# Spreading a norm's inverse root over the partitions: a transpose of the repeated column in place of a product with the identity

## The chip, the core and the metric

The kernel runs on one core of a Trainium2 chip. The metric is device time in microseconds (us) of one execution, the median over several runs. Lower is better.

## The reference, cut to what matters

Three residual blocks of a language model run one after the other on 256 tokens of width 1024: a state-space mixer, a latent-attention mixer, and a block with sparse attention, a gated convolution, a feed-forward part and a per-layer gate. Every block begins with a root-mean-square norm, and there are more norms inside:

```python
def rms_norm(x, w):
    xf = x.astype(jnp.float32)
    return (xf * lax.rsqrt(jnp.mean(xf * xf, axis=-1, keepdims=True) + RMS_EPS)).astype(x.dtype) * w

def reference(x, ...):
    h = x
    h = h + ssd_mixer(rms_norm(h, norm_w[0]), ...)   # 8 grouped norms of its own inside
    h = h + mla_mixer(rms_norm(h, norm_w[1]), ...)   # one norm of the queries, one of the keys
    x = rms_norm(h, final_norm_w)
    ...                                              # sparse attention, conv with layer norm, ffn, gate
    return rmsnorm(h, g_final)
```

The change touches only how the inverse root of a norm gets to where it is multiplied in. No weight, no activation and no other product is touched.

## The kernel before, in words

Activations lie feature-major: a tile is 128 features (partitions) by 256 tokens (columns), and 1024 features are eight such tiles. The weights stream through the core once, in slabs of eight 128x128 blocks (512 KB). SyncE loads a slab into `raw` (six buffers), ScalarE rounds it to `wh` (line 1122), GpSimd takes the rest, `wl = raw - wh` (line 571, six buffers each), and TensorE multiplies. A `project` on TensorE is, for each block of 128 input features, three products of a 128x128 block with 128x256 activations: lines 628, 629 and 630 (high by high, high by low, low by high). Eight such blocks make one output tile of the usual kind. Lines 635 to 637 do the same with the activations as the stationary side. Vector and scalar engines take each output out of PSUM, where three banks rotate, and prepare the next inputs.

Each engine's program is written out by hand, in one fixed order, with semaphores between the engines. TensorE's waits are on `wl_ready` (the slab is there), `proj_done` and the evacuation counts (the bank is free), and on the results of the small steps between the projections.

A norm needs one number for each token, while tokens lie along the columns of every partition. It goes like this:

- `norm_sum` on TensorE (line 655; `group_sum`, line 665, for the grouped norms): the squares are summed over the partitions, with the squares as the stationary side, which leaves one column of 128 sums for each half of the tokens, with the token on the partition.
- `inverse_root` on VectorE (lines 1589 to 1592, then 1567 to 1572): a Newton iteration for the inverse root of that column, in `root` (128 partitions, one column for each half of the tokens; `root1` and `late_tok` for two of the norms).
- `norm_spread` on TensorE (line 673): the column is repeated 128 times as the stationary side, the identity `ident` (in the tile `cst`) is the moving side, and the result holds the root of token j in column j of every partition. This is done for each half of the tokens, into PSUM.
- VectorE either copies it to `late` (line 1604), which later multiplies projection outputs, or multiplies it in at once (line 1557).

`norm_spread` is called 17 times, once with four columns (the last of the grouped norms, which holds two groups) and otherwise with two, so for 36 columns. Sixteen of the calls stand between products of a projection or of an attention stage: for six grouped norms it comes right after `head_out` (lines 756 and 757), in nine other places between ordinary work, and once with four columns within the first state-space output projections. The seventeenth comes at the end of the program (`n_fin2`), where nothing is left to project. There the same column is spread a second time, into another bank (line 1094), for ScalarE: it copies that to `late` (line 1533), GpSimd multiplies the last two of eight output tiles with it (line 589), and VectorE multiplies the first six with the first copy (line 1557). SyncE then stores the eight tiles in four transfers (line 560), the pair of GpSimd third and VectorE's last pair fourth.

Several other places of this kernel turn a 128x128 f32 tile with `nc.tensor.transpose`, which has the tile as the stationary side and the same identity as the moving side: lines 724 (`x_transpose`), 863 (`prob_transpose`), 931 (the gates), 997 (`unit_transpose`) and 1017 (`cmp_transpose`).

Of the kernel before, what the change touches and what calls it, by code (L numbers as in the profile page):

```python
# [18 lines left out]
P = 128  # L19
# [247 lines left out]
def build(nc, slabs_dram, vec_dram, const_dram, x_dram, p_dram, out_dram):  # L267
# [6 lines left out]
    with ctx:  # L274
        def sb(name, shape, dt=f32):
            return ctx.enter_context(nc.sbuf_tensor(name, shape, dt))
# [15 lines left out]
        msq, root, step = sb("msq", [P, 2 * TB]), sb("root", [P, 2 * TB]), sb("step", [P, 2 * TB])  # L292
# [4 lines left out]
        ident = cst[:, 0:128]  # L297
# [103 lines left out]
        PS_TR, PS_S, PS_Y, PS_M = psum[3], [psum[4], psum[5]], psum[6], psum[7]  # L401
# [47 lines left out]
        def sem(name):  # L449
            if name not in sems:  # L450
                sems[name] = ctx.enter_context(nc.semaphore(name))
            return sems[name]
# [140 lines left out]
        def _(pe):  # L593
# [75 lines left out]
            def norm_spread(n):  # L669

                pe.wait_ge(sem("norm_root"), n.i + 1)
                for b in range(n.groups * TB):
                    ins = nc.tensor.matmul(n.rstd[:, b * P:(b + 1) * P], n.root[:, b:b + 1].broadcast_to([P, P]), ident,  # L673
                                           start=True, stop=True)
                ins.then_inc(sem("norm_spread"), 1)

            def norm(n):
                norm_sum(n)
                norm_spread(n)
# [21 lines left out]
            for c in range(SSM_CT):  # L701
                project(f"xbc{c}", u, u_lo)
                if c == 0:
                    norm_sum(n_ssm)
                elif c == 1:
                    pe.wait_ge(sem("const_in"), 16)
                    norm_spread(n_ssm)
                if c == 19:

                    pe.wait_ge(sem("dt_scan"), 8)  # L710
                    pe.wait_ge(sem("masks"), 1)
                    for i, src in enumerate((dtT, acr)):
                        for b in range(TB):
                            o = PS_TR[:, (2 * i + b) * SSM_H:(2 * i + b + 1) * SSM_H]
                            ins = nc.tensor.transpose(o, src[0:SSM_H, b * P:(b + 1) * P], ident[0:SSM_H, 0:SSM_H])
                    ins.then_inc(sem("dt_tr"), 1)
# [48 lines left out]
            for j in range(SSM_PAIRS - 1):  # L765
                project(f"sz{j + 1}", u, u_lo)
                if j % 2:
                    cb_scores((j + 1) // 2)
                x_transpose(j + 1)
                decay_pair(2 * j + 2)  # L770
                head_out(2 * j)
                head_out(2 * j + 1)
                if j % 2 and j >= 3:

                    wait(pe, "cb_evac", (j + 3) // 2)
                    group_sum((j - 3) // 2)
                if j % 2 == 0 and j >= 4:
                    norm_spread(n_grp[(j - 4) // 2])
# [151 lines left out]
            for b in range(TB):  # L930
                ins = nc.tensor.transpose(PS_TR[:, b * P:(b + 1) * P], gT[:, b * P:(b + 1) * P], ident)
# [9 lines left out]
            for n in range(2):  # L941
                ins = nc.tensor.transpose(PS_TR[:, n * P:(n + 1) * P], hg[:, n * P:(n + 1) * P], ident)
# [144 lines left out]
            for b in range(TB):  # L1087
                c = slice(b * P, (b + 1) * P)
                nc.tensor.matmul(PS_M[:, b:b + 1], n_fin2.sum[:, c], ones[:, 0:1], start=True, stop=False)
                ins = nc.tensor.matmul(PS_M[:, b:b + 1], n_fin2.sqb(KD - 1)[:, c], ones[:, 0:1], start=False, stop=True)  # L1090
            ins.then_inc(sem("norm_sum"), 1)
            norm_spread(n_fin2)
            for b in range(TB):
                ins = nc.tensor.matmul(PS_TR[:, b * P:(b + 1) * P], root[:, b:b + 1].broadcast_to([P, P]), ident,
                                       start=True, stop=True)
            ins.then_inc(sem("final_spread"), 1)


# [1244 lines left out]
```

## Time and profile before

| | |
|---|---|
| median of 3 runs | 867.47 us (866.96 to 868.33) |
| span of the profiled execution, first to last instruction | 865.4 us, so the median is 2.1 us above it |
| TensorE busy | 847.8 us, 98% of the span, 7055 products |
| VectorE, ScalarE, GpSimd busy | 526.8, 485.7, 624.1 us |
| mean granted TensorE clock | 0.994 of full speed |

The profiled execution has no device time of its own listed beside its span; what lies around the span is taken as those 2.1 us. A matmul's end in the profile is modelled and products overlap in the pipeline, so what a product costs in a stream is the distance between the starts of products and not the duration of one.

### The profile page before, as it was taken

Reading aid. Unit: us, or ns where it says so; the run is one execution under the profiler, and the core shown is the slowest. Engines: PE = TensorE matmul, PEld = TensorE weight load, DVE = VectorE, ACT = ScalarE, POOL = GpSimd, SP = SyncE. Lnnn points to the kernel's source line nnn. Section 1 sums busy time; section 2 is a strip of 40 time slices with the busy share of each in tenths; the row PEclk is TensorE's granted clock in tenths of the full one; section 3 lists DMA queues with packets and bytes.
Section 4 is the critical chain, followed back from the end, with each engine's and each line's share of the span. In section 5 each row is a group of like instructions: output and inputs, shape, how many; then the busy total and the mean of one; then the engine's idle time right before and its main releaser. Section 6 shows DMA issues by size and latency. Waiting matters only on the chain.

```text
span 865.4 us, 18278 instructions
## 1 busy us (share of the span) xinstructions
PE 847.8 (98%) x7055; PEld 816.2 (94%) x7055; DVE 526.8 (61%) x1543; ACT 485.7 (56%) x925; POOL 624.1 (72%) x282
## 2 busy tenths in 40 slices
PE   8999999999999999999999999999999999999995
PEld 8999988889998899999999999988999999999995
DVE  5997758883243535445458998875566676641164
ACT  6755476664446456563846457875644544554361
POOL 4899756655997455563979899455868888889680
PEclk9999999999999999999999999999999999999997
DMA  8666633332774343433566577433646666667511
GB/s 331 192 219 218 193 99 98 99 98 75 220 218 155 114 145 107 140 99 122 162 204 190 180 210 222 127 95 116 184 144 204 177 192 182 187 193 221 170 49 50
DMA packets 38678, 138.46 MB, mean 160 GB/s; under 512 B 4416, under 2 KB 4544, under 8 KB 38592
## 3 DMA queue, kind: packets, MB, share of 16 engines
q1 hardware_dynamic: 38592, 137.30, 51.9%
q8 instruction: 56, 0.92, 0.5%
q14 instruction: 30, 0.25, 0.1%
HBM read 136.23 MB, written 1.05 MB: 159 GB/s over the span
## 4 chain that ended last, share of the span: by engine, by line
PE 80%; DVE 4%; issue 2%; ACT 1%; POOLq 0%; POOL 0%; ACTq 0%; DVEq 0%
PE ps L628 22%; PE ps L629 22%; PE ps L630 21%; DVE ps L1720 1%; PE ps L850 1%; PE ps L756 1%; PE ps L673 1%; PE ps L655 1%; PE ps L637 1%; PE ps L635 1%; PE ps L636 1%; PE ps L874 1%; PE ps L983 1%; PE ps L846 1%; PE ps L821 1%
## 5 line engine op out<-in xcount | busy, mean ns | idle before, releaser
L571 POOL TENSOR_TENSOR wl<-raw,wh 128x1024 fp32r<-128x1024 f32 x254 | 606.9, 2413 | 199.1 <-ACT wh L1122 198.9
L628 PE MATMUL ps<-uh,wh 128*128 128x256 f32 (+1 forms) x1248 | 352.4, 282 | 1.9 <-POOL wl L571 0.8
L629 PE MATMUL ps<-ul,wh 128*128 128x256 f32 (+1 forms) x1248 | 348.7, 279 | 0.0
L630 PE MATMUL ps<-uh,wl 128*128 128x256 f32 (+1 forms) x1248 | 348.3, 279 | 0.0
L1122 ACT ACTIVATE wh<-raw 128x1024 fp32r<-128x1024 f32 (+1 forms) x255 | 262.9, 1052 | 85.8 <-PE ps L630 77.9
L628 PEld LDWEIGHTS ps<-uh,wh 128*128 128x128 f32 (+1 forms) x1248 | 233.8, 187 | 3.7 <-issue 1.6
L629 PEld LDWEIGHTS ps<-ul,wh 128*128 128x128 f32 (+1 forms) x1248 | 233.7, 187 | 0.0
L630 PEld LDWEIGHTS ps<-uh,wl 128*128 128x128 f32 (+1 forms) x1248 | 233.2, 187 | 0.1
L1813 DVE TENSOR_TENSOR h<-ps,h 128x256 f32<-128x256 f32 x32 | 13.6, 425 | 103.8 <-PE ps L630 103.7
L629 PE MATMUL ps<-ffl,wh 128*128 128x256 f32 x176 | 49.3, 280 | 0.0
L628 PE MATMUL ps<-ffh,wh 128*128 128x256 f32 x176 | 49.1, 279 | 0.0
L630 PE MATMUL ps<-ffh,wl 128*128 128x256 f32 x176 | 49.1, 279 | 0.0
L1720 DVE SCALAR_TENSOR_TENSOR ps<-cpad,vec,ps 128x256 f32<-128x256 f32 x120 | 48.6, 480 | 0.0
L1611 DVE TENSOR_TENSOR fraw<-ps,late 128x256 f32<-128x256 f32 x44 | 18.4, 421 | 38.7 <-PE ps L630 38.6
L1720 DVE SCALAR_TENSOR_TENSOR ps<-sraw,vec,ps 128x256 f32<-128x256 f32 x96 | 38.9, 478 | 0.0
L1720 DVE SCALAR_TENSOR_TENSOR ps<-fraw,vec,ps 128x256 f32<-128x256 f32 x88 | 38.1, 481 | 0.0
L628 PE MATMUL ps<-ynh,wh 128*128 128x256 f32 x128 | 36.1, 282 | 0.0
L628 PE MATMUL ps<-ogh,wh 128*128 128x256 f32 x128 | 36.1, 282 | 0.0
L630 PE MATMUL ps<-ynh,wl 128*128 128x256 f32 x128 | 35.8, 280 | 0.0
L629 PE MATMUL ps<-ynl,wh 128*128 128x256 f32 x128 | 35.7, 279 | 0.0
L630 PE MATMUL ps<-ogh,wl 128*128 128x256 f32 x128 | 35.7, 279 | 0.0
L629 PE MATMUL ps<-ogl,wh 128*128 128x256 f32 x128 | 35.6, 278 | 0.0
(363 smaller groups left out, 1690.8 us busy)
## 6 DMA issues: line engine op xcount, KB each, us to landing
raw<-slabs SPq DMA_DIRECT2D x255, 512.0 KB, 4.0
h<-x_fm SPq DMA_DIRECT2D x4, 256.0 KB, 4.1
out_fm<-outb SPq DMA_DIRECT2D x4, 256.0 KB, 2.2
cst<-shape_consts SPq DMA_DIRECT2D x1, 768.0 KB, 8.4
vec<-vectors SPq DMA_DIRECT2D x1, 299.5 KB, 8.6
pin<-p_fm SPq DMA_DIRECT2D x1, 256.0 KB, 3.8
raw<-slabs SPq DMA_DIRECT2D x1, 128.0 KB, 2.8
vec<-vectors SPq DMA_DIRECT2D x1, 4.0 KB, 2.4
```

The costliest lines, as they stand in the source:

```text
L571: nc.gpsimd.tensor_tensor(wl[:, s % PART_RING, :], raw[:, s % RAW_RING, :], wh[:, s % PART_RING, :].bitcast(f32), ALU.subtract).then_inc(s ...
L628: nc.tensor.matmul(res, w_h, a_h, start=first, stop=False)
L629: nc.tensor.matmul(res, w_h, a_l, start=False, stop=False)
L630: ins = nc.tensor.matmul(res, w_l, a_h, start=False, stop=last)
L635: nc.tensor.matmul(res, a_h, w_h, start=first, stop=False)
L636: nc.tensor.matmul(res, a_h, w_l, start=False, stop=False)
L637: ins = nc.tensor.matmul(res, a_l, w_h, start=False, stop=last)
L655: ins = nc.tensor.matmul(PS_M[:, n.col + c:n.col + c + 1], src[:, b * P:(b + 1) * P], ones[:, 0:1], start=n.summed or k == g * per, stop=n ...
L1122: nc.scalar.activation(wh[:, s % PART_RING, 0:n], raw[:, s % RAW_RING, 0:n], ACT.Copy)\
L1611: tt(dst, o[0:rows, 0:T], late[0:rows, :], ALU.mult).then_inc(sem("dve_evac"), 1)
L1720: return stt(dst, src, w, dst, ALU.mult, ALU.add)
L1813: tt(h[:, k, :], o[:, 0:T], h[:, k, :], ALU.add).then_inc(sem("dve_evac"), 1)
```

## The change

Both places that spread a root over the partitions call `nc.tensor.transpose` in place of `nc.tensor.matmul`. The operands are the same: the repeated column is the stationary side, the identity the moving side, the same slice of PSUM the result. No wait, no semaphore and no other instruction changes, and each engine's instructions keep their order.

```diff
@@ norm_spread
                 pe.wait_ge(sem("norm_root"), n.i + 1)
                 for b in range(n.groups * TB):
-                    ins = nc.tensor.matmul(n.rstd[:, b * P:(b + 1) * P], n.root[:, b:b + 1].broadcast_to([P, P]), ident,
-                                           start=True, stop=True)
+                    ins = nc.tensor.transpose(n.rstd[:, b * P:(b + 1) * P], n.root[:, b:b + 1].broadcast_to([P, P]), ident)
                 ins.then_inc(sem("norm_spread"), 1)
@@ the end of the program
             norm_spread(n_fin2)
             for b in range(TB):
-                ins = nc.tensor.matmul(PS_TR[:, b * P:(b + 1) * P], root[:, b:b + 1].broadcast_to([P, P]), ident,
-                                       start=True, stop=True)
+                ins = nc.tensor.transpose(PS_TR[:, b * P:(b + 1) * P], root[:, b:b + 1].broadcast_to([P, P]), ident)
             ins.then_inc(sem("final_spread"), 1)
```

## Rows read from the trace of the kernel before

**Rows 1.** The page: the span, and TensorE's busy time, share and products.

```profile
span 865.4 us, 18278 instructions
PE 847.8 (98%) x7055; PEld 816.2 (94%) x7055; DVE 526.8 (61%) x1543; ACT 485.7 (56%) x925; POOL 624.1 (72%) x282
```

**Rows 2.** Busy time by stage: stretch, length, busy us (xcount) by engine, clock, DMA.

```profile
530.00:852.00 322.00, 320.88 (x2741) 313.36 (x2740) 187.97 (x556) 176.54 (x330) 239.89 (x101) 1.00 0.53 158
852.00:865.40 13.40, 3.75 (x18) 3.27 (x16) 6.27 (x26) 2.01 (x5) 1.41 (x2) 0.59 0.21 79
```

**Rows 3.** TensorE's groups by form: line, names, shape, xcount, busy us, mean ns, idle before.

```profile
L673 PE MATMUL ps<-cst,root 128*128 128x128 f32 x68 | 11.4, 294 | 2.5 <-DVE root L1572 2.5
...
L863 PE MATMUL ps<-cst,pn 128*128 128x128 f32 x48 | 7.9, 272 | 0.0
...
L1094 PE MATMUL ps<-cst,root 128*128 128x128 f32 x4 | 1.1, 421 | 0.0
...
L673 PE MATMUL ps<-cst,late_tok 128*128 128x128 f32 x4 | 0.6, 273 | 0.0
```

**Rows 4.** TensorE in order of time, a spread (L673) within a projection: start, us.

```profile
18.27 0.28 PE L630 MATMUL ps<-uh,wl 128*128 128x256 f32 x1
18.39 0.60 PE L673 MATMUL ps<-cst,root 128*128 128x128 f32 x4
...
18.95 0.28 PE L629 MATMUL ps<-ul,wh 128*128 128x256 f32 x1
```

**Rows 5.** TensorE in order of time, two transposes (L931) between projections.

```profile
499.54 0.28 PE L630 MATMUL ps<-uh,wl 128*128 128x256 f32 x1
499.66 0.38 PE L931 MATMUL ps<-cst,gT 128*128 128x128 f32 x2
...
500.00 0.28 PE L636 MATMUL ps<-wl,cxh 128*128 128x256 f32 x1
```

**Rows 6.** A spread right after head_out (L757), the last of six.

```profile
189.32 0.71 PE L673 MATMUL ps<-cst,root 128*128 128x128 f32 x4
...
190.00 0.28 PE L629 MATMUL ps<-ynl,wh 128*128 128x256 f32 x1
```

**Rows 7.** Three transposes (L997) right after f32 products with 64 columns (L1010).

```profile
594.00 0.55 PE L997 MATMUL ps<-cst,npn 128*128 128x128 f32 x3
...
594.50 0.28 PE L629 MATMUL ps<-cnl,wh 128*128 128x256 f32 x1
```

**Rows 8.** TensorE's waits from 19 to 852 us: who for whom, us, times, longest.

```profile
PE ps L635 <- POOL wl L571: 0.8, 2, 0.6
...
PE ps L628 <- POOL wl L571: 0.8, 1, 0.8
...
PE ps L846 <- ACT qn L1299: 0.5, 1, 0.5
```

**Rows 9.** ScalarE and GpSimd around the wait for weights at 514 us.

```profile
505.78 0.38 ACT L1389 ACTIVATE hg<-ps 64x256 f32<-64x256 f32 x1 [2.69 <-PE ps L637]
...
507.18 21.28 POOL L571 TENSOR_TENSOR wl<-raw,wh 128x1024 fp32r<-128x1024 f32 x9 [1.05 <-ACT wh L1122]
```

**Rows 10.** All engines in order of time at the end of the program.

```profile
858.11 1.22 PE L673 MATMUL ps<-cst,root 128*128 128x128 f32 x4 [2.50 <-DVE root L1572]
...
859.12 1.06 PE L1094 MATMUL ps<-cst,root 128*128 128x128 f32 x4
859.37 2.44 DVE L1557 SCALAR_TENSOR_TENSOR outb<-h,vec,ps 128x256 f32<-128x256 f32 x6 [1.32 <-PE ps L673]
860.22 0.38 ACT L1533 ACTIVATE late<-ps 128x256 f32<-128x256 f32 x1 [5.50 <-PE ps L1094]
860.27 2.65 SPq L560 DMA_DIRECT2D out_fm<-outb  x4
860.68 1.41 POOL L589 TENSOR_TENSOR outb<-outb,late 128x256 f32<-128x256 f32 x2 [16.23 <-ACT late L1533]
```

**Rows 11.** DMA rate in 40 slices of 0.1225 us from 860.5 to 865.4.

```profile
GB/s 0 0 0 0 17 351 334 418 334 368 284 167 435 334 385 418 351 84 0 50 318 351 401 351 451 335 368 401 368 435 351 101 0 0 0 0 0 0 0 0
```

## The prediction, made before the changed kernel was run

> **What bounds the kernel now.** I read the page first. TensorE is busy for 847.8 of 865.4 us [rows 1], so the question is whether a product taken out of its stream shortens the program, and by how much. The view by stages says where it does: from 530 to 852 us TensorE is busy for 320.88 of 322 us, while VectorE has 187.97 and GpSimd 239.89; at the end, from 852 to 865.4 us, it is busy for only 3.75 of 13.40 us at a granted clock of 0.59 [rows 2]. The first is a stream in which every product counts. The second is a chain of short steps through four engines, in which only what lies on the chain counts.
>
> Then I read the groups of TensorE by form. The spread of a root is in the profile as 68 + 4 records at line 673 and 4 at line 1094 [rows 3]. The program has 36 columns at the first and 2 at the second, so **one f32 product of a column with the identity is two records**. The turning of the attention weights (line 863) is written as three transposes for each of 16 heads, 48 in all, and has 48 records [rows 3]: **one f32 transpose of the same shape is one record**, of nearly the same duration (272 ns, against 273 for the spread of `late_tok`). Duration is latency in a pipeline, so it is not the price. The price is read from the order of time.
>
> **The price of a spread in the stream.** In [rows 4] the last product before the spread starts at 18.27, and the second product behind it at 18.95: 0.68 us for one step to the spread, four records, and one product of line 628. In [rows 5] the same distance with two transposes between is 499.54 to 500.00, 0.46 us. The difference is 0.22 us for two records less, so 0.11 us for a record of either form. The neighbours are of the same kind in both places, and whatever a switch between ordinary products and transposes costs, and the same loading of weights behind them, is in both numbers.
>
> The 16 calls within the stream:
>
> - Nine calls with two columns stand between ordinary products: 9 x 0.22 = 1.98 us.
> - Six calls with two columns come right behind the f32 products of `head_out`. There the distance from the first spread record to the second product behind is 189.32 to 190.00 = 0.68 us [rows 6]. The nearest row of the other kind is three transposes behind f32 products of the sparse attention, 594.00 to 594.50 = 0.50 us [rows 7]; with one record less that is 0.39. The difference is 0.29 us. The lower bound is the 0.22 of the plain case. I take 0.26, between the two, because the products in front are of the same shapes but not the same line: 6 x 0.26 = 1.56 us. Bounds 1.3 and 1.7.
> - One call with four columns has eight records, and loses four of them: 4 x 0.11 = 0.44 us.
>
> Together 3.98 us. In a stream that waits for nothing this comes off the end in full.
>
> **Does something else take it back?** TensorE's waits between 19 and 852 us are few: the longest are 0.8 us in total for weights twice over (lines 635 and 628 for `wl`), and 0.5 us for a copy of ScalarE [rows 8]. A wait keeps what was saved before it if the work waited for was itself started by TensorE. For the weights this is so: GpSimd runs nine slabs without a pause from 507.18 us, and it began when ScalarE gave it a slab, and ScalarE had stood still for 2.69 us until TensorE's projection `hk` was done, at 505.78 [rows 9]. So the run of nine begins earlier by all that TensorE has saved until then, and the wait moves with it. The waits for ScalarE's and VectorE's copies are of outputs that TensorE has just made, and move too. I take nothing off, and keep a loss as a rival. The spread is also nobody's only cover: VectorE, which waits for it, gets it 0.22 us sooner, never later.
>
> **The end of the program.** Here the root is ready, and the spreads run at the lower clock (0.59 on average [rows 2], 421 ns for a record of line 1094 against 273 [rows 3]). Four records of line 673 begin at 858.11 and four of line 1094 at 859.12 [rows 10]. The second group ends at 859.12 + 1.06 = 860.18, and one of its records lasts 0.42, so the last begins at 859.76: three steps in 0.64, 0.213 us each. The path behind is: ScalarE's copy at 860.22, GpSimd's two products from 860.68 to 862.09, and the third and fourth stores [rows 10]. Four records fewer stand in front of that path: 4 x 0.213 = 0.85 us. VectorE's path has two fewer: 0.43 us, so that its six products end at 861.81 - 0.43 = 861.38, and GpSimd's at 862.09 - 0.85 = 861.24. The third store can go then, and the fourth follows it, as now.
>
> The transfers have to fit as well. They run at 0.1225 us to a slice: from slice 4, 861.0, to slice 17, 862.6, for the first two stores; a pause of about 0.3 us; then until about 864.4 [rows 11]. The first two begin 0.43 us earlier, at 860.6, and end at 862.2; the last two are ready 0.85 us earlier, at about 862.1, so the pause closes to nearly nothing and the end comes 0.8 us earlier. Bounds: 0.43 us if the stores are tied to VectorE alone, 0.85 if the transfers never touch. I take 0.8.
>
> **The sum.** 3.98 + 0.8 = 4.8 us off the span of 865.4, so 860.6. The median of the runs shown lies 2.1 us above that span, and the change does nothing to what lies around it: 867.47 - 4.8 = 862.7 us.
>
> **A rule of the Trainium skill against the row.** The row says that a transpose costs one record of 0.11 us where the product costs two, half [rows 4, 5]. The Trainium skill, in "TensorE: Matmul & The Clock Gate" (the table of terms, the entry on xbus), speaks of a transpose mode that is four times faster for FP32. By it a spread would shed three quarters of its price and not half. No row of this trace shows that: the transposes already here are at 0.11 us for a column of the spread's shape.
>
> **The rivals.**
>
> - *As summed* (0.85): 862.7 us; its own range 861.9 to 864.0. The bounds of the six calls give 0.3 less or 0.1 more, the end 0.4 less; the noise of a median, from the spread of the runs, is about 0.5 either way; and part of the saving may be lost at a wait.
> - *A quarter and not a half* (0.03): a column would go from 0.22 to 0.055 us in the stream. The 34 columns there save 0.165 each, 5.6 us, and the end would have 4 columns at a quarter of 0.43, so 1.28 us off GpSimd's path, of which the transfers let through about 0.9. The time would be 861.0. Against it stand the transposes of [rows 5] and [rows 7]. It is what the rule named above would give. It would have to be that a stationary side of one repeated column loads faster than 128 different ones.
> - *The stream gives it back* (0.05): the weights bind at 507 to 528 us not by TensorE's release but by their own rate, from far earlier. Then all that was saved before goes: six of the nine plain calls, the six grouped ones and the four columns, 1.32 + 1.56 + 0.44 = 3.3 us. What is left is 3 x 0.22 + 0.8 = 1.5 us: 866.0 us. For it speaks that TensorE does wait for `wl` there [rows 8]; against it, that GpSimd itself had waited 1.05 us just before [rows 9].
> - *Slower, by the repeated column* (0.04): no transpose in this trace has a stationary side with a step of zero; all have 128 different columns. If the transposing form reads such a side badly, each of 34 columns is dearer in the stream. It decides at twice the transposed record, 0.22 us. At 0.44 us a column the stream would grow by 34 x 0.22 = 7.5 us, and the end by nearly 1: 876 us. Against it: as a product the same repeated column steps at 0.11 us a record, like all others [rows 4].
> - *The change isn't made* (0.03): for a repeated column the call gives the same pair of records, and the time stays at 867.5. Against it stands only that every f32 transpose here has one record.
>
> **How the numbers follow.** About 0.2% (1.7 us) is what a measurement of this kernel can tell from no change. The first two cases are faster: 0.88. The third, at 1.5 us, and the last are within the bound: 0.08. The fourth is slower: 0.04. The range holds the first case with its losses and reaches to the second: 861.0 lies outside at 0.03, and 864.5 on the upper side leaves out 0.12 of the rivals and a little of the first.
>
> **What the profile of the changed kernel would show.** Line 673 with 36 records and line 1094 with 2, at about 272 ns at full clock. The distance from the last product before a plain spread to the second behind it at 0.46 us. The fall of the first call behind `head_out` from 0.68 to between 0.39 and 0.46. TensorE's waits from 19 to 852 us as many and as long as now, with GpSimd's run of nine slabs beginning 3.3 us earlier than 507.18. At the end, GpSimd's first product 0.85 us closer behind the root than the 2.57 us of now (858.11 to 860.68), and the transfers without a pause. The prediction would be wrong if a record of the new form steps at more than 0.11 us, if the waits for `wl` grow by what was saved, or if TensorE's clock falls or rises elsewhere at the end: at the full clock all eight records there would take 0.11 us each, and the saving would be half of 0.85; at the lower clock for more of the sums before, a few tenths of a us would be lost.

## The result, and the profile after

The changed kernel took 858.72 us, the median of four runs, against 867.82 us for four runs of the kernel before: a ratio of 0.9895, with a 95% interval of 0.9862 to 0.9928. That is faster, as forecast, but by 9.1 us and not by 4.8, and the time lies below the stated range. The four runs are also far apart, as those of the kernel before are not:

```
changed kernel   855.02  856.79  860.65  862.41
kernel before    866.96  867.47  868.17  868.33
```

First, what answers to the rows that the sum was made of. TensorE's groups by form show each f32 column as one record, 36 at line 673 and 2 at what is now line 1093, as against [rows 3]:

```profile
L673 PE MATMUL ps<-cst,root 128*128 128x128 f32 x34 | 6.9, 291 | 2.5 <-DVE root L1570 2.5
...
L1093 PE MATMUL ps<-cst,root 128*128 128x128 f32 x2 | 0.6, 421 | 0.0
...
L673 PE MATMUL ps<-cst,late_tok 128*128 128x128 f32 x2 | 0.4, 270 | 0.0
```

TensorE in order of time, at the spread ahead of the feed-forward part: from the last product before it to the second behind it are 0.45 us (638.94 to 639.39), for the 0.68 of [rows 4].

```profile
638.94 0.28 PE L630 MATMUL ps<-uh,wl 128*128 128x256 f32 x1
639.06 0.38 PE L673 MATMUL ps<-cst,root 128*128 128x128 f32 x2
...
639.39 0.28 PE L629 MATMUL ps<-ul,wh 128*128 128x256 f32 x1
```

The same view at the last spread behind `head_out`: 188.47 to 188.86, 0.39 us for the 0.68 of [rows 6], so 0.29 was the price there, the upper of the two bounds.

```profile
188.47 0.43 PE L673 MATMUL ps<-cst,root 128*128 128x128 f32 x2
...
188.86 0.28 PE L629 MATMUL ps<-ynl,wh 128*128 128x256 f32 x1
```

And all engines at the end of the program. GpSimd begins 850.23 - 848.62 = 1.61 us behind the first spread, for 2.57 in [rows 10], and the span ends 6.4 us behind it for 7.3:

```profile
848.62 0.69 PE L673 MATMUL ps<-cst,root 128*128 128x128 f32 x2 [2.50 <-DVE root L1570]
...
849.10 0.63 PE L1093 MATMUL ps<-cst,root 128*128 128x128 f32 x2
...
849.77 0.38 ACT L1531 ACTIVATE late<-ps 128x256 f32<-128x256 f32 x1 [4.09 <-PE ps L1093]
850.23 1.41 POOL L589 TENSOR_TENSOR outb<-outb,late 128x256 f32<-128x256 f32 x2 [14.70 <-ACT late L1531]
```

So every term of the sum is there, and the stores now follow one another: the DMA rate has no slice at nothing between them. What is not in the sum is found by laying the starts of the same spreads side by side (first column the kernel before, from the order of time of both):

```
start of the spread, us          before   after   difference  gained since the row above
first (state-space block)         18.39   19.38     +0.99
attention block                  245.25  244.05     -1.20        2.19
sparse block                     451.12  449.27     -1.85        0.65
feed-forward part                640.89  639.06     -1.83       -0.02
gate part                        828.37  819.48     -8.89        7.06
last                             858.11  848.62     -9.49        0.60
end of the span                  865.4   855.0     -10.4         0.91
```

The first two stretches gave what was summed: 0.22 + 6 x 0.26 + 0.44 = 2.2 us and 3 x 0.22 = 0.66 us. (The 0.99 us of the first row have nothing to do with the spreads. The 40 records of warm-up products ahead of everything, which the change doesn't touch, take 6.33 us in the kernel before and 7.15 in the changed one. Eight of their records step there at 0.21 us in place of 0.11, which is how records step at the lower clock at the end of the program, though the profile gives a granted clock of 1.00 for this stretch in both.) But the feed-forward part, in which one spread of 0.22 us was shortened, became 7.06 us shorter. The view by stages shows how. It lists TensorE's busy time with the number of products (x), the granted clock, and the share and rate of the DMA. This is the kernel before:

```profile
403.00:413.00 10.00, 10.00 (x91) 10.00 (x90) 6.74 (x12) 2.62 (x6) 0.00 (x0) 1.00 0.20 54
430.00:440.00 10.00, 10.00 (x87) 10.00 (x86) 3.48 (x8) 5.40 (x9) 10.00 (x5) 1.00 0.74 231
650.00:750.00 100.00, 100.00 (x851) 100.00 (x851) 66.60 (x175) 49.71 (x72) 83.96 (x36) 1.00 0.64 192
```

And this the changed one:

```profile
430.00:440.00 10.00, 10.00 (x87) 10.00 (x86) 2.21 (x6) 3.69 (x8) 10.00 (x6) 1.00 0.76 227
455.00:475.00 20.00, 20.00 (x179) 20.00 (x178) 19.45 (x45) 11.33 (x18) 20.00 (x9) 1.00 0.72 214
650.00:750.00 100.00, 100.00 (x884) 100.00 (x884) 70.41 (x185) 50.26 (x75) 87.75 (x38) 1.00 0.65 196
```

TensorE is 100% busy in all six, at the full clock, with products of the same shapes. Yet in the same 100 us it does 851 of them in one kernel and 884 in the other: one every 117.5 or every 113.1 ns. **The projection stream has two rhythms**, and keeps one of them through dozens of projections. Start to start, a product takes 117.8 ns (they come as 118, 117 and 119) or 113.3 ns (113 and 114). From the spread ahead of the feed-forward part to the one behind it the stream has 44 projections of 24 products and 8 of 66, 1584 in all. The last 27 come behind the sums of squares for the next norm, at 815.75 us, and are slow again. The other 1557, at 4.45 ns each, are worth 6.9 us, and with the 0.22 of the spread that is the 7.06 of the stage within 0.1. The kernel before has the fast rhythm too, at 403 us for instance (91 products in 10 us, against 87 at 430). It was in the trace, and I had not looked for it. There are other patterns: from 604 to 634 us, in every profile of this document, six steps of 125, 116, 123, 118, 121 and 117 ns repeat, 120.0 on average. And a rhythm need not last until the next instruction of another kind. The fast one of 401 us ends within its stream, at a single step of 154 ns (the product of line 629 at 415.87 us here), and does so in all twelve profiles in which that stream starts fast, behind the same product. GpSimd has finished a slab of `wl` just before (413.18 + 2.41 = 415.59), so this may be a short wait for it; the profile names none.

### The profile page after: what moved, and what is told of

It is laid out like the page before. It is cut to its first block, busy times and chain, and to the rows that moved or that the text cites. A ratio compares the mean times of both kernels' runs of the same rounds, so it can differ in the third digit from the quotient of the medians.

```text
span 855.0 us, 18202 instructions
## 1 busy us (share of the span) xinstructions
PE 836.3 (98%) x7017; PEld 804.1 (94%) x7017; DVE 528.0 (62%) x1543; ACT 485.7 (57%) x925; POOL 624.4 (73%) x282
## 4 chain that ended last, share of the span: by engine, by line
PE 78%; DVE 6%; ACT 1%; issue 1%; DVEq 0%; ACTq 0%
PE ps L628 21%; PE ps L630 21%; PE ps L629 21%; DVE ps L1718 3%; PE ps L849 1%; PE ps L755 1%; PE ps L635 1%; PE ps L655 1%; DVE cx L1982 1%; PE ps L636 1%; PE ps L637 1%; PE ps L873 1%; PE ps L845 1%; PE ps L982 1%; PE ps L820 1%
```

## The experiments

Where the runs of a kernel fall into groups, its times are listed, since a median of two groups says little. "The kernel before" ran beside them all, 100 executions in the end; but for one at 909.19, which is left out as disturbed, all lie from 866.57 to 869.76.

### The changed kernel once more

No edit.

> The changed kernel once more, five rounds and a new profile. Its first profile shows two rhythms of the projection stream: a product starts every 117.8 ns or every 113.3 ns, and the feed-forward stage (639 to 819 us) was wholly in the fast one, where the kernel before was wholly in the slow one. Theory A (the rhythm is drawn anew in each execution at the entry to a stage): times spread over 855 to 863 us again, and the profile may show another rhythm in another stage; the span is 860.5 minus what the fast rhythm gives over its own stages. Theory B (the new form of the spread itself makes the stage behind it fast, always): all times within 1 us, and the same fast stages. Theory C (the first four runs were spread by something outside the program, such as the chip): the kernel before spreads as widely on the same chip.

Measured, against 23 runs of the kernel before on the same chip (median 867.62): ratio 0.9887, interval 0.9864 to 0.9911.

```
856.26 856.28 856.32 856.36 856.91 863.26
```

With the first four, that is ten runs: seven from 855.0 to 856.9, one at 860.65, two above 862. The new profile, of a run at 856.28, had the feed-forward stage in the fast rhythm again (884 products from 650 to 750). Theory B falls, since some runs are slow; C falls, since the kernel before was steady beside it. A is left: each execution draws. (Which stage was slow in the runs above 862 is read here from their times; no profile was taken of them.)

### Only the norm ahead of the feed-forward part

```diff
+                    if n is n_ffn:
+                        ins = nc.tensor.transpose(dst, col, ident)
+                    else:
+                        ins = nc.tensor.matmul(dst, col, ident, start=True, stop=True)
```

(`dst` and `col` are the slice of PSUM and the repeated column, as before.)

> The kernel before, with the transposing form only in the one norm ahead of the feed-forward part (2 columns). By the products removed alone it should be 0.22 us faster: 867.5. Theory A (rhythm drawn at the entry to the stage): in some executions 7 to 8 us faster, about 860, in others 867.5, nothing much between. Theory B (the form makes the next stage fast): 860 in all. Rival (the feed-forward stage's rhythm is set by something further up): 867.5 in all.

```
860.01 860.21 860.24 860.51 861.27 861.90 862.21 866.68 866.89 867.28 867.55 868.23
```

Two groups, seven runs near 861 and five near 867.3. Two records taken from 7000 are worth 0.22 us or about 7. The profile is of the run at 862.21, and has the fast rhythm in that stage; its row for it:

```profile
650.00:750.00 100.00, 100.00 (x885) 1.00 0.65 193
```

### All norms but that one

```diff
+                    if n is not n_ffn:
+                        ins = nc.tensor.transpose(dst, col, ident)
+                    else:
+                        ins = nc.tensor.matmul(dst, col, ident, start=True, stop=True)
```

> The changed kernel, with only the norm ahead of the feed-forward part spread by the product as before. Theory A and B (the rhythm of the feed-forward stage is set where that stage is entered): no execution below 861, 862 to 863.2 in most, so the width of the times shrinks to 1 to 2 us. Rival (any change of phase further up sets it): times from 855 to 863 as for the full change.

Measured 862.96 us (five runs, 862.21 to 863.87), ratio 0.9947, interval 0.9935 to 0.9958. In its profile the feed-forward stage is slow:

```profile
650.00:750.00 100.00, 100.00 (x852) 1.00 0.61 188
```

This kernel has all of the sum but 0.22 us, for which the prediction's arithmetic gives 862.9. So the work that is saved is worth about what was summed, and the rest comes from one stage whose rhythm changes with what is done where it is entered.

### Only the norm at the end

```diff
+                    if n is n_fin2:
+                        ins = nc.tensor.transpose(dst, col, ident)
+                    else:
+                        ins = nc.tensor.matmul(dst, col, ident, start=True, stop=True)
```

The edit is made to the changed kernel, so the second copy for ScalarE stays a transpose.

> The kernel before, with the transposing form only in the last norm, behind the whole stream (4 columns at the lower clock). The sum of the prediction gives 0.8 us less, 0.9 by the changed kernel's profile: 866.7 in all executions, with the narrow spread of the kernel before. If the times of this kernel are wide too, the form of the spreads is not what widens them.

Measured 866.43 us (11 runs, 865.81 to 868.10) against 867.62: 1.2 us less, ratio 0.9990, interval 0.9981 to 0.9998. Narrow, as expected. The difference of medians is 0.4 above the 0.8 of the sum, which the interval (0.2 to 1.6 us) holds.

### What opens the fast rhythm: three other bursts

All three leave the kernel before as it is but for what stands at the spread ahead of the feed-forward part. A burst is what comes between two projections there, in records. The three edits are put together here and shortened.

```diff
-                for b in range(n.groups * TB):   # two products, 4 records
+                for b in (0, 1, 0, 1):           # first kernel: transposes, 4 records
+                for b in (0, 1, 0, 1):           # second kernel: products, 8 records
+                for b in (0,):                   # third kernel: a product, 2 records,
+                ins = nc.tensor.transpose(n.rstd[:, P:2 * P], ...)   # and a transpose, 1 record
```

> The kernel before, with each of the two columns ahead of the feed-forward part transposed twice: four records of the transposing form where four of the product stood, so that nothing is taken out of the stream. Theory form (a burst of transposes can leave the stream behind it in the fast rhythm, a burst of such products does not): two groups of times, about 867.6 and about 860, though no work is saved. Theory count (what matters is that two records are fewer, so that the stream is entered at another moment): 867.6 in all, as narrow as the kernel before.

> The kernel before, with each of the two columns ahead of the feed-forward part spread twice by the product: eight records for four, 0.44 us of work more. Theory form: 868.1 in all and never near 860. Theory count or phase (any other length of the burst enters the stream at another moment and draws a new rhythm): some executions near 860.5.

> The kernel before, with the first of the two columns ahead of the feed-forward part spread by the product and the second by the transpose: two product records and then one transposing record, 0.11 us less work. If what counts is the form of the last record ahead of the stream: two groups of times, 867.5 and 860. If it takes two transposing records, or the burst's length: 867.5 in all.

Measured: 867.35 us for four transposing records (11 runs, 867.11 to 868.47), 868.20 for eight of the product (11 runs, 867.59 to 869.41), 867.45 for three (11 runs, 867.07 to 868.58). The kernel before had 867.77 beside them. None of the 33 runs is below 867. My theory that the transposing form opens the fast rhythm has fallen with the first of them: twice as many transposes, and it never comes. What the kernel with two groups had, and these had not, is a burst of two records. That can be tried with either form.

### A burst of two products, and a burst of one transpose

```diff
+                for b in (0,) if n is n_ffn else range(n.groups * TB):
```

Both spread only the first half of the tokens' roots there; what is left out is said in the expectations.

> The kernel before, with only the first of the two columns ahead of the feed-forward part spread, by the product: two product records where four stood. The inverse root of the second half of the tokens is left out there, so that half is scaled by what lies in PSUM. If the number of records ahead of the stream is what opens the fast rhythm: two groups of times, 867.4 and 860, as for two transposing records. If it has to be two records of the transposing form: 867.4 in all.

```
859.77 860.45 860.77 861.01 866.70 866.88 866.90 866.97 867.39 867.41 867.80 867.93
```

Four of twelve runs in the fast group, without a transpose anywhere near. (The groups are told by the times: the one profile, of the run at 867.41, is slow, with 852 products from 650 to 750 us.) So it is not the form of the instruction.

> The kernel before, with only the first of the two columns ahead of the feed-forward part spread, by the transpose: one transposing record where four product records stood; the second half of the tokens is scaled by what lies in PSUM. By the records removed 867.3. Theory phase (each length and form of the burst enters the stream at its own moment, and only some moments open the fast rhythm): nothing certain, either one group at 867.3 or two; a group near 859.7 shows that it needs no pair.

Measured 867.26 us, 11 runs from 866.88 to 868.10, one group. At this place one, three, four, six (below) and eight records never opened the fast rhythm, in 60 runs (16 of them below) and those of the kernel before; two did, in 18 of 34 runs with either form (seven of ten, seven of twelve, four of twelve). The chip is not the cause: on each of the chips of the kernels with one, three, four and eight records, a kernel with two had two groups of times beside them.

The profiles hold a second place of this kind. The second of the two spreads at 451 and 454 us has four records in ten of the sixteen profiles of this document, and none of the ten is fast behind it (172 or 173 products from 455 to 475 us). It has two records in the six others, and five of these are fast there (179 products). In the sixth, that of the kernel with more bursts below, the spread at 449.49 us had opened the fast rhythm and the one at 452.44 ended it.

Two is not the right length everywhere, though. The three transposes of line 863 at 302.30 us open the fast rhythm in the kernel before (39 products at 113.3 ns behind them), and in 12 of the 13 profiles in which they come behind a slow stream; the same three come six more times before 397 us in the kernel before, and leave the stream slow each time.

### Idle transposes right behind the spread

```diff
+                if name == "fg1":
+                    for c in range(2):
+                        nc.tensor.transpose(outs[0][:, c * P:(c + 1) * P], ident, ident)
```

> The kernel before with nothing taken out, and two idle transposes of the identity put in ahead of the second gate projection of the feed-forward part (into the PSUM bank of that projection, which overwrites it). 0.22 us of work more. Theory rhythm (two transposing records in the slow stream open the fast one in part of the executions): two groups of times, 867.9 and about 860.5, so that a kernel with more work is faster. Rival (the fast stage comes only with the spread itself as a transpose): 867.9 in all.

> The changed kernel with the same two idle transposes ahead of the second gate projection of the feed-forward part. There the stream is in the fast rhythm already in about two thirds of the executions. In the profiles a burst of transposes met in the fast rhythm was followed by the slow one in 12 of 13 cases. Theory rhythm: most executions fall back, times near 863, median 862 to 863, though only 0.22 us of work is added; some stay or come to 857. Rival (the fast rhythm, once there, holds the stage): 856.5 as the changed kernel, plus 0.2.

The place was not what these texts say. The spread is called right before the projection `fg1`, so the idle pair joined it: a burst of six records in the first kernel and of four in the second, and not a burst of its own in a running stream. Read so, both fit what was found above. The first measured 868.04 us (11 runs, 866.79 to 868.25), with no fast group. The second measured 862.56 us, and its five runs lie within 0.4 us (862.22 to 862.59), ratio 0.9942, interval 0.9930 to 0.9954: the changed kernel with 0.22 us of work more, all slow in the feed-forward stage by their times, and in the profile of one.

```profile
650.00:750.00 100.00, 100.00 (x851) 1.00 0.62 189
```

Less the 0.22 us, this is 862.3 for the full change without the fast stage, where the sum said 862.7.

### A pair of idle transposes by itself

The same lines, for `fg2`, 24 + 24 products further on.

> The kernel before with two idle transposes ahead of the third gate projection of the feed-forward part, 5.7 us behind the spread, so that they are a burst of two records of their own in the slow stream (in the run before this they stood right behind the spread's four records and made a burst of six). 0.22 us of work more, nothing taken out. Theory rhythm (a burst of two records in the slow stream can open the fast rhythm): two groups of times, 867.8 and about 860.5. If it is the spread's own place that matters and not a burst of two: 867.8 in all.

> The changed kernel with the same two idle transposes ahead of the third gate projection, 5.4 us behind the spread. Here they meet the fast rhythm in about two thirds of the executions. Theory rhythm (any burst ends the run of the fast rhythm, and a burst of two in the slow one can open it): executions that were fast fall to 862.5, some that were slow rise to 856.7; the median is above 860. Rival (once fast, the stage stays fast): 856.5 in most, as the changed kernel, plus 0.2.

In the kernel before: 868.25 us, 11 runs from 867.47 to 869.88, one group. A pair in the slow stream does not open the fast rhythm wherever it stands; my theory expected two groups. In the changed kernel: 863.34 us, five runs from 862.17 to 863.77, none fast. That half of it held, and the order of time shows it happen. Here lines 631 to 633 are the projection and line 610 the idle pair:

```profile
643.89 0.28 PE L631 MATMUL ps<-uh,wh 128*128 128x256 f32 x1
...
644.45 0.28 PE L633 MATMUL ps<-uh,wl 128*128 128x256 f32 x1
644.57 0.38 PE L610 MATMUL ps<-cst 128*128 128x128 f32 x2
...
645.02 0.28 PE L633 MATMUL ps<-uh,wl 128*128 128x256 f32 x1
...
645.97 0.28 PE L632 MATMUL ps<-ul,wh 128*128 128x256 f32 x1
```

Before the pair six steps take 0.68 us (643.89 to 644.57), 0.113 each. Behind it eight take 0.95 (645.02 to 645.97), 0.119 each. The fast stream met a burst of 0.22 us, and 1509 products behind it are slow, which is 6.7 us. That is the rule and not a special case: in all sixteen profiles 93 bursts of 2 to 32 records come between a fast stream and another (of nine products or more), and behind 89 of them the stream is no longer fast.

### More bursts in stages that are slow

```diff
+            def redraw():
+                for _ in range(2):
+                    nc.tensor.transpose(PS_TR[:, 3 * P:4 * P], ident, ident)
             for c in range(SSM_CT):
+                if c == 8:
+                    redraw()
...
+            redraw()
             for n in range(SO_FIRST, KD):
```

> The changed kernel with two bursts of two idle transposes of the identity (into a piece of PSUM that nothing reads) in stages that have been slow in all profiles: ahead of the ninth state-space input projection (47 to 104 us) and ahead of the fourth output projection (217 to 242 us). The bursts cost 4 x 0.11 = 0.44 us and, where the draw comes out, give 500 and 210 products back at 4.45 ns each, 2.2 and 0.9 us. Theory draw: the lowest times fall under the lowest of the changed kernel (855.0) to 853 to 854.5, the median by less than 1 us. Rival (these stages can't be fast, whatever stands ahead): 0.4 us slower than the changed kernel.

```
856.68 856.90 857.51 858.20 863.13 863.33
```

Median 857.85 us, ratio 0.9901, interval 0.9875 to 0.9926. The lowest is not below that of the changed kernel, so nothing shows that the bursts opened anything. Its profile is of the run at 863.33. The streams behind both bursts stay at 117.8 ns in it, and the feed-forward stage is slow, with 852 products from 650 to 750 us. By the times, four of these six runs were fast in that stage, behind a spread of two records as in the changed kernel, so that the count above becomes 22 of 40.

This profile has one thing more to say. Here is the entry to the stage that came out slow:

```profile
638.57 0.28 PE L630 MATMUL ps<-uh,wl 128*128 128x256 f32 x1
638.69 0.38 PE L673 MATMUL ps<-cst,root 128*128 128x128 f32 x2
638.82 0.36 PE L628 MATMUL ps<-uh,wh 128*128 128x256 f32 x1
639.02 0.28 PE L629 MATMUL ps<-ul,wh 128*128 128x256 f32 x1
```

The distances are those of the changed kernel's entry that came out fast, 0.12 and 0.33 us (638.94, 639.06, 639.39 there). So the same burst with the same steps leads to either rhythm.

## Why the prediction was wrong, point by point

**What held.** The pricing of a record by the distance between products held: 0.23 us for a plain spread where 0.22 was said, and 0.29 behind `head_out`, where I took 0.26. The first two stretches gained 2.19 and 0.65 us, for 2.22 and 0.66. The end gave 0.91 us in the profile, for 0.8 and an upper bound of 0.85. The waits for weights moved along: GpSimd's long run began at 505.18 us instead of 507.18, close to the 1.85 us that this execution was ahead at 451 us. I had said 3.3 us earlier; most of the difference is its late start, 0.99 us behind at the first spread. The kernels in which the feed-forward stage stays slow stand at 862.96, 862.56 and 863.34 us, for a forecast of 862.7 with 0.2 us more for each.

**Where that agreement is luck in part.** In the first stretch the spreads gave 2.35 us (0.28 at each of the six behind `head_out`), and one wait took 0.28 of it back: TensorE's wait for VectorE's `gb` at 192 us is 0.6 us long, for 0.3 before. The prediction had the waits for VectorE move along with TensorE, and took nothing off:

```profile
PE ps L756 <- DVE gb L1795: 0.3, 1, 0.3
PE ps L755 <- DVE gb L1793: 0.6, 1, 0.6
```

In the gate part 0.60 us were gained where one spread of 0.22 was shortened. The last sums of squares did the rest: from the first of them to the last spread are 858.11 - 854.06 = 4.05 us in the kernel before and 848.62 - 845.03 = 3.59 in the changed one, since records of them step at 0.21 us in the first (two from 854.62 to 855.04) and at 0.11 in the second (two from 845.47 to 845.69). The granted clock from 854.60 to 855.30 is 0.50, and from 845.40 to 846.10, the same records, 0.82. The prediction named a clock that falls elsewhere at the end as a sign against it, and it did fall elsewhere.

```profile
854.62 0.56 PE L1089 MATMUL ps<-ones,sqsum 128*128 128x1 f32 x2
855.04 0.56 PE L1090 MATMUL ps<-ones,sq 128*128 128x1 f32 x2
...
845.47 0.36 PE L1088 MATMUL ps<-ones,sqsum 128*128 128x1 f32 x2
845.69 0.43 PE L1089 MATMUL ps<-ones,sq 128*128 128x1 f32 x2
```

**What failed** is the step of the prediction that reads: "In a stream that waits for nothing this comes off the end in full." It takes it for granted that the products which are left cost what they cost before. They don't: each costs 117.8 or 113.3 ns, by the rhythm of its stage, and 1557 of them hang on one entry, which was worth 6.9 us in the profile of the changed kernel. None of the rivals had this. The one that was faster than the forecast, a record at a quarter of the price, did not happen (a transposing record steps at 0.11 us). For the spread from run to run I had taken "about 0.5 either way" from the kernel before, whose entry to that stage always came out slow.

**Part of the fast rhythm is given back.** From 451 to 641 us the change should have brought 0.66 us (three spreads) and the fast rhythm from 453 to 480 us a further 1.0 us, at 179 products in 20 us for 172. The stretch gained nothing. VectorE, with its convolution, is 19.45 us of 20 busy there, and TensorE's waits in that stretch have two that were not there before:

```profile
PE ps L628 <- DVE nq L1966: 0.2, 1, 0.2
PE ps L635 <- DVE ksT L1991: 0.2, 1, 0.2
```

By the starts of the products those two gaps are 514 and 488 ns long, and with the longer step behind each they cost 0.95 us. The remainder, about 0.7 us, matches stretches that were fast in the kernel before and slow in this one (489 to 499.5 us, and 531.5 to 537, 545 to 548 and 554 to 556.6): the starts give 0.3 us for the first and 0.4 for the others. That remainder is read from the two traces and was not tried by itself.

**What stays open.** Why two rhythms exist, and what at the entry decides between them, isn't settled. The experiments say that it is neither the removed work alone (one record in place of four, which removes more than two do, never opened it) nor the form. What the other engines do can't be what holds a rhythm, since both last for some 180 us beside the same loads; whether it has a say at the entry was not tried. Nor is the length of the burst enough: two records at 639 us lead to either rhythm with the same steps, the same pair does nothing 5 us further on in the slow stream, and three records open the fast one at 302 us. That suggests that the moment of entry, against some slower beat, is what counts. The experiments don't show such a beat.

## What to carry to other kernels

Price an instruction in a stream by the distance between its neighbours' starts, in two places that differ only in it; here that was right to half a microsecond in 5, with some luck, as terms of 0.3 to 1 us that nobody had summed cancelled. But before such a sum is trusted, count the products in equal stretches of the trace: where equal work at equal clock and full busy share shows two counts (here 87 and 91 in 10 us), the stream has a second speed, an edit that cuts into it may flip a whole stage, and a range has to hold that. And run such a change more than a few times: medians of four here hid two groups 6 us apart, and whether this edit is worth 5 us or 11 in one execution is drawn anew each time.

## What the runs showed of the hardware that had not been expected

- A projection of 128x128 by 128x256 products steps at 117.8 or 113.3 ns at the full granted clock (one stage of this kernel at 120.0), and keeps its rhythm for up to 180 us.
- A burst of two records (0.22 us, products or transposes) ahead of one stage opened the fast rhythm in 18 of 34 executions, 22 of 40 with those of the kernel with more bursts; bursts of 1, 3, 4, 6 and 8 at the same place in none. Elsewhere three records opened it too (302 us).
- A pair of idle transposes in the fast stream ended it at once, and so did a single step of 154 ns, for 113, in twelve profiles.
- A transpose of an f32 column repeated 128 times is one record that steps at 0.11 us in the stream and at 0.21 us at the lower clock (the two of line 1093 take 0.63 us from 849.10, and one lasts 0.42); the product of the same operands is two. The repeated column costs the transposing form nothing extra.
